# Expert rows scattered into a table in token order, and the loop over pairs of blocks in three groups

## The reference

```python
def hier_moe(h, w_rg, b_rg, w_re, b_re, w_up, w_down):
    grp = jnp.argmax(h @ w_rg + b_rg, axis=-1)
    ...
    top_v, top_i = lax.top_k(logit_e, TOP_K)
    gate = jax.nn.softmax(top_v, axis=-1) * p_grp
    expert = (grp[:, None] * EXPERTS_PER_GROUP + top_i).reshape(-1)
    order = jnp.argsort(expert)
    ...
    def expert_block(args):
        xb, e = args
        g, u = jnp.split(xb @ w_up[e], 2, axis=-1)
        return (jax.nn.silu(g) * u) @ w_down[e]

    y = lax.map(expert_block, (buf.reshape(n_blocks, MOE_BLOCK, D), blk_expert)).reshape(-1, D)
    y = y[dest] * gate.reshape(-1)[order][:, None].astype(h.dtype)
    return jax.ops.segment_sum(y, tok_sorted, num_segments=n_tok)
...
x = x + mod[:, 5] * hier_moe(h2)
return rms_norm_2(x, final_g)
```

## Time and profile before

| | us |
|---|---|
| median of 3 runs | 2901.03 |
| lowest and highest | 2896.57, 2902.46 |
| profiled execution, its own time | 2889.24 |
| its span | 2887.4 |
| TensorE busy in the span | 2759.5 |
| VectorE, ScalarE, GpSimd busy | 1506.3, 777.0, 79.0 |

### The profile page before, as it was taken

One profiled execution on the slowest core, in us unless ns is written; L12 is line 12 of the kernel. 1 busy time (PEld: TensorE's weight loads), 2 busy tenths in 40 slices (PEclk: granted clock), 3 DMA queues, 4 the chain that ended last, 5 costly groups with the idle time before them and its releaser, 6 DMA issues. The chain is left out here.

```text
span 2887.4 us, 44114 instructions
## 1 busy us (share of the span) xinstructions
PE 2759.5 (96%) x18251; PEld 1644.2 (57%) x18251; DVE 1506.3 (52%) x2115; ACT 777.0 (27%) x1444; POOL 79.0 (3%) x106
## 2 busy tenths in 40 slices
PE   8999889999999999999999989999998899999985
PEld 4444554444444444444454445656564899999974
DVE  7886676566666668773642008856765111111103
ACT  2111771111111115412100016756423121112111
POOL 0000000000000000000000000000000000000022
PEclk9999999999999999999999999999999899999997
DMA  3022842111111127763231000022202999999992
GB/s 143 31 73 40 264 175 73 44 44 44 44 44 44 44 67 280 265 245 111 71 90 44 8 11 1 1 59 88 75 7 75 375 402 406 409 410 405 405 359 79
DMA packets 82614, 422.65 MB, mean 146 GB/s; under 512 B 13504, under 2 KB 23232, under 8 KB 66496
## 3 DMA queue, kind: packets, MB, share of 16 engines
q1 hardware_dynamic: 58528, 362.29, 34.1%
q10 hardware_dynamic: 15664, 41.95, 4.0%
q0 software_dynamic: 8304, 16.79, 1.8%
HBM read 393.07 MB, written 51.38 MB: 154 GB/s over the span
## 5 line engine op out<-in xcount | busy, mean ns | idle before, releaser
L3605 PE MATMUL ex_up_ps<-big,ex_xT 128*32 128x128 f32 x3072 | 349.1, 274 | 0.0
L3603 PE MATMUL ex_up_ps<-big,ex_xT 128*32 128x384 f32 x3072 | 344.8, 490 | 0.7 <-ACT ex_xT L3690 0.6
L3605 PEld LDWEIGHTS ex_up_ps<-big,ex_xT 128*32 128x32 f32 x3072 | 334.3, 110 | 0.6
L1758 PE MATMUL ffn_ps<-h,V 128*128 128x512 f32 x504 | 219.7, 592 | 0.0
L2217 PE MATMUL ffn_ps<-big,V 128*128 128x512 f32 x484 | 211.3, 597 | 3.7 <-DVE V L2472 1.4
L3603 PE MATMUL ex_y_ps<-ex_wd,ex_hT 128*32 128x384 f32 x1536 | 180.9, 493 | 5.1 <-issue 4.3
L296 DVE TENSOR_SCALAR_CACHE_REDUCE h<-ad_s_ps 128x1280 f32<-128x1280 f32 x64 | 92.9, 1489 | 172.7 <-PE ad_s_ps L205 172.7
L3605 PE MATMUL ex_y_ps<-ex_wd,ex_hT 128*32 128x128 f32 x1536 | 178.8, 276 | 3.0 <-issue 2.9
L3605 PEld LDWEIGHTS ex_y_ps<-ex_wd,ex_hT 128*32 128x32 f32 x1536 | 169.0, 111 | 7.2 <-issue 6.5
L1758 PEld LDWEIGHTS ffn_ps<-h,V 128*128 128x128 f32 x504 | 95.8, 190 | 120.5 <-issue 120.5
L2217 PEld LDWEIGHTS ffn_ps<-big,V 128*128 128x128 f32 x484 | 92.2, 191 | 120.4 <-issue 114.5
(11 more groups left out here) (603 smaller groups left out, 4799.0 us busy)
## 6 DMA issues: line engine op xcount, KB each, us to landing
big<-in_w_eup SPq DMA_DIRECT2D x64, 2048.0 KB, 20.9
ex_wd<-in_w_edown SPq DMA_DIRECT2D x32, 2048.0 KB, 20.7
V<-in_w_down SPq DMA_DIRECT2D x35, 704.0 KB, 5.6
dn_tail<-in_w_mod ACTq DMA_DIRECT2D x48, 512.0 KB, 5.4
fm_up<-in_w_up SPq DMA_DIRECT2D x22, 1028.0 KB, 4.9
y_dram<-in_cos SPq DMA_DIRECT2D x1, 21504.0 KB, 71.5
y_dram<-big ACTq DMA_DIRECT2D x32, 288.0 KB
dn_tail<-in_w_in SPq DMA_DIRECT2D x17, 512.0 KB, 4.6
```

What stands on the lines that cost most here:

```text
L1758: mm = nc.tensor.matmul(bank(i, j), wj[:, k, :], bj[:, k, :], start=(k == 0), stop=(k == 3))
L3603: nc.tensor.matmul(o[32 * g:32 * g + 32, 0:W], rows(g), w[:, 0:W], start=first, stop=last)
L3605: mm = nc.tensor.matmul(o[BR:P, g * P:(g + 1) * P], rows(g), w[:, W:BANK], start=first and g == 0, stop=last and g == GR - 1)
```

## The change

In `route`, the two rows of a token get an order: the row of the expert with the lower number is row t of `y_dram`, the other is row 1024 + t (`swapped`, `code`). `y_dram` has 2048 rows now. The code travels through the same matmuls as the token number did; `ids` (for the gather) and `rows` (for the scatter) come out of it. `early` and `late` are gone.

```diff
+                st.done(V_.tensor_tensor(swapped, first_at, c1, ALU.is_gt))
+                for a in range(2):
+                    st.done(V_.tensor_scalar(code[:, a], swapped, float(T) * (1 - 2 * a), float(T) * (a - 2), ALU.mult, ALU.add))
+                    st.done(V_.tensor_tensor(code[:, a], code[:, a], cst["token"], ALU.add))
...
-                    st.done(V_.scalar_tensor_tensor(out=here, in0=wide(cst["token"], NB), scalar=-float(T), in1=here,
-                                                    op0=ALU.add, op1=ALU.mult))
+                    st.done(V_.tensor_tensor(here, wide(code[:, a], NB), here, ALU.mult))
...
-                V_.tensor_scalar(r["ids"][0:BR, 0:NB], ids_ps[0:BR], float(T), None, ALU.add).then_inc(ids_kept, 1)
-                st.done(V_.tensor_scalar(blkf, lanef, 1.0 / 16, -0.498, ALU.mult, ALU.add))
...
+                st.done(V_.tensor_scalar(flag[0:BR], ids_ps[0:BR], -float(T), -float(T), ALU.is_ge, ALU.mult))
+                V_.scalar_tensor_tensor(out=r["ids"][0:BR, 0:NB], in0=ids_ps[0:BR], scalar=2.0 * T, in1=flag[0:BR], op0=ALU.add,
+                                        op1=ALU.add).then_inc(ids_kept, 1)
+                V_.tensor_scalar(r["rows"][0:BR, :], ids_ps[0:BR], 2.0 * T, None, ALU.add)
```

In `experts`, ACT no longer stores y. It moves the last quarter of each row (kept in partitions 96 to 127) beside the rest, in three DMAs within SBUF (`move_y`), and POOL scatters the 96 rows to their places with an indirect DMA (`scatter`), waiting for it to land:

```diff
-                def store_y(i, u):
+                def move_y(i, u):
                     act.wait_ge(y_kept, i * 2 + (u + 2))
-                    dst = y_dram[bass.ds(i * 2 + u, 1)].rearrange("a p n -> (a p) n")
-                    act.dma_start(dst[:, 0:2 * W], y[0:BR, u]).then_inc(stored[u], 16)
-                    act.dma_start(dst[:, 2 * W:D].rearrange("(g p) n -> p g n", g=GR),
-                                  y[BR:P, u].rearrange("p (g n) -> p g n", g=GR)).then_inc(stored[u], 16)
+                    for g in range(GR):
+                        act.dma_start(y[32 * g:32 * g + 32, u, 2 * W:D], y[BR:P, u, g * 2 * P:(g + 1) * 2 * P]).then_inc(moved[u], 16)
...
+                def scatter(i, u):
+
+                    nc.gpsimd.tensor_copy(row_at[0:BR, u:u + 1], r["rows"][0:BR, bass.ds(i * 2 + u, 1)]).then_inc(row_set, 1)
+                    pool.wait_ge(row_set, i * 2 + (u + 2))
+                    pool.sem_inc(pool_seen, 1)
+                    pool.wait_ge(moved[u], i * (16 * GR) + 16 * GR)
+                    pool.sem_inc(pool_seen, 1)
+                    pool.indirect_dma_start(y_dram, bass.IndirectOffsetOnAxis(ap=row_at[0:BR, u:u + 1], axis=0), y[0:BR, u, :], None,
+                                            bounds_check=2 * T - 1, oob_is_err=False).then_inc(stored[u], 16)
+                    pool.wait_ge(stored[u], i * 16 + 16)
+                    pool.sem_inc(y_free, 1)
```

The loops of all five engines become an outer loop of 3 groups and an inner one of 9 passes, with a test before each group and before each pass (here POOL's, with its two new calls):

```diff
-                with pool.Fori(1, NB // 2) as i:
-                    with pool.If(i * 2 < nb):
-
-                        pool.wait_ge(turned, i * 2 + 1)
-                        gather(i, 1, i * 2)
-                        pool.wait_ge(turned, i * 2 + 2)
-                        gather(i + 1, 0, i * 2 + 1)
...
+                with pool.Fori(0, GROUPS) as o:
+                    with pool.If(o * (2 * GROUP) + 2 < nb):
+                        with pool.Fori(0, GROUP) as j:
+                            i = pool.snap(o * GROUP + j + 1)
+                            with pool.If(i * 2 < nb):
+
+                                pool.wait_ge(turned, i * 2 + 1)
+                                gather(i, 1, i * 2)
+                                pool.wait_ge(turned, i * 2 + 2)
+                                gather(i + 1, 0, i * 2 + 1)
+                                scatter(i - 1, 0)
+                                scatter(i - 1, 1)
```

```diff
+                for f, got, a in ((f0, got0, 0), (f1, got1, 1)):
+                    sp.wait_ge(up_done, pairs * 2 + (a + 1))
+                    sp.wait_ge(y_free, pairs * 2 + (a + 1))
+                    for t in (4, 0, 5, 1, 6, 2, 7, 3) if a == 0 else range(TT):
+                        sp.dma_start(f[:, t, :], y_dram[a * T + t * P:a * T + (t + 1) * P, :]).then_inc(got[t], 16)
+                for t in range(TT):
+                    sp.wait_ge(finished, t + 1)
+                    sp.dma_start(out[t * P:(t + 1) * P, :], f1[:, t, :]).then_inc(out_stored, 16)
...
-                sp.dma_start(y_dram.rearrange("(b p) n -> p b n", p=P),
-                             din["cos2"].unsqueeze(1).to_broadcast([P, NB * BR // P, T])).then_inc(y_filled, 16)
```

More of the change, by code:

```diff
@@ L2673 @@
 NBI = NB + 1
-FAR = 8192
+ROWS = 7
+GROUP, GROUPS = 9, 3
 TT = T // P
@@ L3161, in route @@
         g4b, begun = carve(TT, 4), carve(E_)
-        c1, low, pg = (carve(TT) for _ in range(3))
+        c1, low, pg, first_at = (carve(TT) for _ in range(4))
+        code = carve(2, TT)
+        std, swapped = r["std"], r["swapped"]
         base, nblk, incl, onesr, total = (carve(E_) for _ in range(5))
@@ L3593, in _ @@
+                pairs = used_pairs(pool)
+                scatter(pairs - 1, 0)
+                scatter(pairs - 1, 1)
             @block.tensor
@@ L3651, in down, with token_sum @@
                     mm.then_inc(y_done, 1)
+                def token_sum(t):
+                    for k in range(KD):
+                        nc.tensor.matmul(sum_ps[t][:, k // 4, k % 4 * P:(k % 4 + 1) * P], h[:, k, t * P:(t + 1) * P], cst["ident"],
+                                         start=(k % 4 == 0), stop=False)
+                    pe.wait_ge(got0[t], 16)
+                    for half in range(2):
+                        mm = nc.tensor.matmul(sum_ps[t][:, half, :], r["diag"][:, t, :], f0[:, t, half * BANK:(half + 1) * BANK],
+                                              start=False, stop=True)
+                    mm.then_inc(summed, 1)
                 turn(0, 0)
@@ new lines, in _ @@
+                for t in range(PET, TT):
+                    dve.wait_ge(scaled, t - PET + 1)
+                    row = rows[:, t % ROWS, :]
+                    nc.vector.scalar_tensor_tensor(out=row, in0=row, scalar=r["std"][:, t:t + 1], in1=f0[:, t, :], op0=ALU.mult,
+                                                   op1=ALU.add).then_inc(added, 1)
+                def mix(t):
+                    if t < PET:
+                        dve.wait_ge(summed, t + 1)
+                        rest = sum_ps[t].rearrange("p a n -> p (a n)")
+                    else:
+                        dve.wait_ge(added, t - PET + 1)
+                        rest = rows[:, t % ROWS, :]
+                    dve.wait_ge(got1[t], 16)
+                    nc.vector.scalar_tensor_tensor(out=f1[:, t, :], in0=f1[:, t, :], scalar=r["gate"][:, 1, t:t + 1], in1=rest,
+                                                   op0=ALU.mult, op1=ALU.add).then_inc(mixed, 1)
@@ L3903, in experts_block @@
         h2_dram = nc.dram_tensor("h2_dram", (T, D), F32).ap()
[L3904 to L3905 removed]
+        y_dram = nc.dram_tensor("y_dram", (2 * T, D), F32).ap()
+        blk, ids, out_rows = keep("blk", [P, NB], I32), keep("ids", [P, NBI], I32), keep("out_rows", [P, NB], I32)
         count, first_expert = keep("count", [P, 2], I32), keep("first_expert", [P, 1], I32)
[L3907 to L3909 removed]
+        small = big[:, 20, 4 * P:4 * P + 9 * TT]
+        r = {"g4": small[:, 0:4 * TT].rearrange("p (t g) -> p t g", t=TT), "top": small[:, 4 * TT:5 * TT],
+             "gate": small[:, 5 * TT:7 * TT].rearrange("p (a t) -> p a t", a=2), "std": small[:, 7 * TT:8 * TT], "swapped": small[:, 8 * TT:9 * TT], "rows": out_rows[:], "block": blk[:], "count": count[:], "ids": ids[:], "first": first_expert[:],
+             "gate5": big[:, 18, 0:8 * BR], "final": big[:, 19, :], "diag": big[:, 20, 0:4 * P].rearrange("p (t n) -> p t n", n=P)}
         wu = big[:, 0:16, :].rearrange("p a n -> p (a n)").rearrange("p (u s k n) -> p u s k n", u=2, s=2, k=KD)
```

305 lines of the change are left out of this document (126 added, 179 removed).

## The result

The changed kernel takes 3054.55 us in the median of 4 runs (3050.59 to 3056.57), the kernel before 2899.24 on the same chip. The ratio is 1.0539, with an interval of 1.0524 to 1.0555. I had forecast slower, at 2968 us with a range to 3050: the direction and the place were right, the size was not.

What follows compares the result with a forecast made beforehand. TensorE and DMA were both taken as full in the expert stage. From 2889.2 us profiled, -36 for the tail and +103 for POOL's queue gave 2956, or 2968 us for the median; range 2885 to 3050.

Steps and rivals of the forecast that it cites:

- the queue of POOL: Expert loop: POOL's wait for each scatter's landing closes a chain with one turn, 7.4 us a pass, +103 us.
- The wait itself then unloads the queues: Expert loop: landings grow in line with the DMA share 34/P, so a pass takes P = 41.4 us.
- M: Loop chain: landing time of ACT's moves, 2.3 us near idle, growing by 5.3 us with the DMA share.
- S: Loop chain: landing time of POOL's scatter, 3.8 us near idle, growing by 6.5 us to 10.3.
- G: Loop chain: landing time of POOL's gather, 3.8 us near idle, growing by 6.5 us to 10.3.
- rival D: Loop: TensorE's clock drops after each wait, 2 us a pass, +28, 2996 us; chance 0.16.
- Rival C: Loop: landings stay slow while weights are queued, 13.3 us of wait a pass, 3051 us; chance 0.12.
- Rival B: Loop: landings total under 17.6 us, passes stay at 34.0 us, 2865 us; chance 0.17 for faster.
- The tail: From the last but one `down` to the end: -36 us together, between -10 and -40.
- The early gathers out of the `down`: Last but one `down`: plain tile loads replace gathers later, 22.15 to 5.25 us, -16.9 us, or 0.
- The tests: Behind the taken passes: 12 skipped passes become 3 and one skipped group, -5.0 us.
- After the last y: End of kernel: last moves, scatter, table loads and combine take 37.7 instead of 54.5 us, -16.8 us.

Runs made afterwards that it cites:

- thin weights: The changed kernel, but in the loop SP loads only a quarter of each gate and up tile (0.5 MB instead of 2 MB): 2864.71 us.

## Why the prediction was right or wrong

**The place and the direction: right.** The term that decides was the queue of POOL. The turns of (i, 1) wait for the gather's landing, the gather follows a scatter, and the closed chain is there piece by piece. Sending the gathers ahead takes the loop from 724.6 to 540.0 us with the same work and the same waits for landings.

**The size of a pass: wrong, and this is the step that failed.** It was the rule that gave the three landings their size: "The wait itself then unloads the queues", and so each grows from its light value in line with the DMA share of the whole pass, 34/P. That gave P = 41.4. A pass took 47.7, so the wait is 13.7 us a pass, not 7.4. Against the sum of 16.4 + M + S + G, in the pass shown:

| term | predicted | measured |
|---|---|---|
| turn to kept y | 12.5 | 14.5 |
| ACT's issues | 1.2 | 1.6 |
| M | 2.3 + 5.3 x 0.82 = 6.6 | 10.4 |
| POOL's start | 0.86 | 0.88 |
| S | 3.8 + 6.5 x 0.82 = 9.1 | 9.2 |
| POOL's step | 1.9 | 1.8 |
| G | 9.1 | 8.9 |

The term that was mis-sized is M: it has 3.8 of the 6.3 us that a pass was longer than forecast. The turn to y has 2.0, which the sum had at nothing and left to rival D, and ACT 0.4. The light value of M, 2.3 us, was about right: the thin weights have 1.8 to 1.9 where almost nothing runs beside the moves. The loaded one was not: 2.3 + 5.3 = 7.6 was the most that the rule allowed at a full share, and the third move lands 10.4 us behind its issue. A single move beside the weights takes 8.4.

The rule was wrong too, even where its number came out. The share does fall, to 0.78, as forecast. But the free time lies in the 8 us behind the turn, where no link of the chain uses the queues. While M, S and G run, the share is 0.94 to 1.05 in M (2801 to 2809 us) and 0.97 over the 22 us that hold M and S. The averaged share was the wrong quantity. S and G came out near their number by luck: at a share of 0.97 the same rule would give 10.1 for each, and they took 9.7 and 8.8 in the mean of the passes. With that share in all three landings the rule would have given 44.0 us a pass, so it accounts for less than half of the miss. The thin weights show that it is the load beside them that makes S slow: it falls to 3.5.

**Rival C** (landings don't shrink) gave 13.3 us a pass and 3051 us; 13.7 and 3054.55 came. It had 0.12 and came nearest. Its three landings were taken at 30.9 us together and have 28.5, so its number is in part luck; the slow clock of rival D and ACT's issues make up the difference. By the Trainium skill, DMA: Bandwidth & Descriptors, Queues, rings and completion order, a DMA engine goes round between its queues a packet at a time. The trace agrees as far as it goes: with weights in flight the depth of SP's queue hardly mattered, since a gather lands after 10.3 us beside weights that take 27.4 us, and after 8.9 us beside weights that take 10.6.

**Rival D** (the clock follows the wait) was right as well, and adds to C: 2 us a pass forecast, 2.0 in the chain from turn to y. The granted clock is 0.62 and then 0.50 in the idle stretch, 0.50 for the first 3.4 us behind it, then 0.90 and 1.00.

**Rival B** (the scatter keeps up) is refuted for this order of the gathers: its three landings had to stay under 17.6 us, and they have 28.5.

**The tail: right.** -35.3 us against -36. The early gathers out of the `down`: 22.15 to 5.24 us, as forecast to 5.25. In all runs the slow `down` goes with them (22.15 to 22.85 us in the three profiles that have them beside it, 5.24 to 5.34 without), but no single change shows it on one chip. The tests: 3.25 us of gap instead of 2.5, and -5.5 us when changed alone, against -5.0. After the last y: 42.0 us, where 37.7 + 3 was forecast; the last moves and scatter took 5.3 and 4.1 us, the moves beside the table loads (2.3 and 3.8 were forecast, and 3 us for both together).

**The fill, routing and all else ahead of the experts: not settled.** I said 0.2 us, and the profiled executions differ by 10.9. But the first turn comes at 2254 to 2261 us in the four profiled executions of kernels with the old routing and at 2256 to 2267 in the ten with the new one, which all have the same code ahead of it. The two sets overlap, and their means are 3.9 us apart; a few us may belong to the change, and the whole of the 10.9 hardly does.

## What to carry to other kernels

When a kernel that keeps its DMA queues full gets a new wait in a loop, follow the chain once around the loop and take each small transfer at a landing time measured beside the weights, of its own kind: M was taken from a light copy and an assumed growth, and of the three landings it was the one far off. A wait lowers the mean DMA share, but the freed time lies behind the wait, not under the transfers of the chain. And ask what a wait has behind it on its engine: sending each gather a pass earlier, in a few lines, was worth 185 us here.

Moving rows between partitions by DMA is dear in such a loop (three moves of 32 KB took 11.9 us and slowed the weights), and an engine that writes to other partitions while it keeps the result did it in 1.31 us.

## What the runs showed of the hardware

- A transfer of 32 KB within SBUF landed after 8.4 us beside 2 MB weight tiles, and after 1.8 to 1.9 us where almost nothing ran beside it. In the thin weights, a gather of 96 rows in the chain landed after 2.8 to 4.0 us and a scatter after 3.5; beside full weights, with the gathers ahead, they took 10.3 and 11.3.
- Waiting in software for a scatter to land cost much less here than its landing time. Without the wait, the gather issued 2.0 us behind it landed 5.8 us after it, 14.0 us after its own issue; the saving was 3.4 of 9.2 us a pass.
- A `down` product of 5.3 us took 22 us in the three profiled executions that had indirect gathers of single rows into SBUF beside it. All three are of chips on which the kernel before takes 2899 us. The plain 512 KB loads that took their place begin at 3008.35, within the last product; from the kept hidden rows to y this takes 8.0 us (3003.81 to 3011.85), and 7.6 us before (2824.30 to 2831.93).
- Chips of one kind differ: the kernel before took 2899 us on one chip and 2869 on two others. The runs of the result also had 2899, and the record doesn't say whether that was a fourth chip. Its loop takes 533 us wherever it was profiled, and where the 30 us lie is open. The version without gathers from the table and without moves took 2858 us on a chip of either kind.
